# A fourth pair of split buffers for the feed-forward, embedding, gated and MLP stages of a two-model forward pass

## What is computed

```
h = h + concat(diff_attention, gated_conv) @ a_w_out          # first model, layer 0
h = h + swiglu(rms_norm(h), ffn_w1, ffn_w3, ffn_w2)           # D_FF = 2816
h = h + sigmoid(rms_norm(h) @ ple_gate[0]) * (p[0] @ ple_proj[0])
u, v = split(gelu(rms_norm(h) @ c_w_in))                      # first model, layer 1
h = h + (u * (w_s @ layer_norm(v) + b)) @ c_w_out
h = h + moe_swiglu(rms_norm(h))                               # top 2 of 8 experts
h = h + sigmoid(rms_norm(h) @ ple_gate[1]) * (p[1] @ ple_proj[1])
for l in range(2):                                            # second model
    h = h + g1 * (concat(swa, mla, nsa, moba)(norm(h) @ w_in[l]) @ w_out[l])
    h = h + g2 * (square(relu(norm(h) @ w_up[l])) @ w_down[l])
```

## Time and profile before

| | |
|---|---|
| median of 3 runs | 1989.69 us (1988.63 to 1994.04) |
| profiled execution, first to last instruction | 1988.3 us |
| PE busy | 1911.1 us (96%) |
| DVE busy | 1555.3 us (78%) |
| ACT busy | 1197.3 us (60%) |
| mean granted TensorE clock | 0.988 of full speed |
| HBM read | 510.14 MB, 257 GB/s over the span |

### The profile page before, as it was taken

One profiled execution on the slowest core, in us unless ns is written; L12 is line 12 of the kernel. 1 busy time (PEld: TensorE's weight loads), 2 busy tenths in 40 slices (PEclk: granted clock), 3 DMA queues, 4 the chain that ended last, 5 costly groups with the idle time before them and its releaser, 6 DMA issues.

```text
span 1988.3 us, 27637 instructions
## 1 busy us (share of the span) xinstructions
PE 1911.1 (96%) x10878; PEld 1646.7 (83%) x10878; DVE 1555.3 (78%) x2130; ACT 1197.3 (60%) x1649; POOL 28.8 (1%) x32
## 2 busy tenths in 40 slices
PE   7999999999999999999999999889899999989998
PEld 7989998777888888888888888679789988978997
DVE  5768887667898989898989899567678985856555
ACT  4544435545777777777777778457554445654443
POOL 0010000000000000000000000000000000000000
PEclk9999999999999999999999999999999999999999
DMA  7348886535999999999989899533258883324551
GB/s 306 128 160 327 327 329 249 197 138 229 341 355 343 355 344 354 344 350 348 356 342 356 341 357 347 220 129 124 88 198 339 346 331 131 125 85 159 191 191 43
DMA packets 71694, 513.08 MB, mean 258 GB/s; under 512 B 8194, under 2 KB 8578, under 8 KB 10114
## 3 DMA queue, kind: packets, MB, share of 16 engines
q1 hardware_dynamic: 69536, 504.40, 67.3%
q10 hardware_dynamic: 2020, 6.82, 1.0%
HBM read 510.14 MB, written 1.05 MB: 257 GB/s over the span
## 4 chain that ended last, share of the span: by engine, by line
PE 88%; DVE 6%; ACT 4%; issue 1%; POOL 1%; DMA 0%; POOLq 0%; SPq 0%; ACTq 0%; DVEq 0%
PE ps L536 27%; PE ps L538 26%; PE ps L537 26%; PE ps L757 2%; DVE w_lo L1375 2%; ACT w_hi L2263 2%; PE ps L945 1%; PE ps L709 1%; PE ps L722 1%; PE ps L963 1%; POOL stat L2768 1%; DMA ring<-in_stream 0%; ACT xT L2273 0%; DVE y_lo L1998 0%; PE ps L992 0%
## 5 line engine op out<-in xcount | busy, mean ns | idle before, releaser
L2263 ACT ACTIVATE w_hi<-ring 128x1024 fp32r<-128x1024 f32 x862 | 911.9, 1061 | 632.7 <-PE ps L538 625.0
L1375 DVE TENSOR_TENSOR w_lo<-ring,w_hi 128x1024 fp32r<-128x1024 f32 x862 | 1041.8, 1223 | 301.4 <-ACT w_hi L2263 278.1
L536 PE MATMUL ps<-w_hi,x_hi 128*128 128x512 f32 (+1 forms) x1056 | 409.4, 390 | 8.8 <-DVE w_lo L1375 3.6
L538 PE MATMUL ps<-w_hi,x_lo 128*128 128x512 f32 (+1 forms) x1056 | 400.1, 381 | 0.0
L537 PE MATMUL ps<-w_lo,x_hi 128*128 128x512 f32 (+1 forms) x1056 | 399.3, 380 | 0.0
L536 PE MATMUL ps<-x_hi,w_hi 128*128 128x256 f32 x1248 | 359.8, 288 | 5.5 <-DVE x_lo L1490 4.5
L537 PE MATMUL ps<-x_lo,w_hi 128*128 128x256 f32 x1248 | 355.3, 285 | 0.0
L538 PE MATMUL ps<-x_hi,w_lo 128*128 128x256 f32 x1248 | 355.0, 284 | 0.0
L536 PE MATMUL ps<-w_hi,h_hi 128*128 128x512 f32 x732 | 289.8, 396 | 2.4 <-DVE h_lo L1983 2.4
L537 PE MATMUL ps<-w_lo,h_hi 128*128 128x512 f32 x732 | 285.3, 390 | 0.0
L538 PE MATMUL ps<-w_hi,h_lo 128*128 128x512 f32 x732 | 284.7, 389 | 0.0
(11 more groups left out here) (280 smaller groups left out, 1401.4 us busy)
## 6 DMA issues: line engine op xcount, KB each, us to landing
ring<-in_stream SPq DMA_DIRECT2D x479, 1024.0 KB, 5.0
con<-in_consts ACTq DMA_DIRECT2D x1, 2048.0 KB, 23.3
arena<-in_ln_rows ACTq DMA_DIRECT2D x3, 512.0 KB, 4.3
resid<-in_x SPq DMA_DIRECT2D x1, 1024.0 KB, 6.2
arena<-in_c ACTq DMA_DIRECT2D x2, 512.0 KB, 3.6
arena<-in_fin_row ACTq DMA_DIRECT2D x2, 512.0 KB, 4.2
out<-rows SPq DMA_DIRECT2D x2, 512.0 KB, 2.6
arena<-in_w_s ACTq DMA_DIRECT2D x1, 512.0 KB, 8.3
```

Source lines behind the costliest of these rows:

```text
L536: pe.matmul(out_, lhs[0], rhs[0], start=start, stop=False)
L538: return pe.matmul(out_, lhs[1], rhs[0], start=False, stop=stop)
L1375: dve.tensor_tensor(lo, ring[:, q % RING, a:a + HALF], hi.bitcast(F32), ALU.subtract)\
L2263: act.activation(half_buffer(m)[0], ring[:, q % RING, a:a + HALF], ACT.Copy).then_inc(hi_ready, 1)
```

## The change

The table `BUFFER` gets four pairs in the ranges of halves `DEEP` instead of in the experts' alone: 32 to 675, 702 to 771 and 798 to 861. In each range pairs are counted from the range's own start. Where a limit of `split_to` was a sum with `PAIRS`, it is now `reach(...)`. DVE gets one wait ahead of the scores of each block, for the last half in the fourth pair.

```
-MOE_PAIRS = 4
+DEEP_PAIRS = 4
+DEEP = (range(2 * W_FFN0, 2 * (W_BLK + B_V)), range(2 * (W_BLK + B_MLP), 2 * (W_BLK + B_ALL + B_V)),
+        range(2 * (W_BLK + B_ALL + B_MLP), 2 * SLOTS))
 def buffers_of_halves():
-    moe = range(2 * W_MOE, 2 * W_PLE1)
-    buffer = [(m - moe.start) % MOE_PAIRS if m in moe else m % PAIRS for m in range(2 * SLOTS)]
+    buffer = [m % PAIRS for m in range(2 * SLOTS)]
+    for stages in DEEP:
+        for m in stages:
+            buffer[m] = (m - stages.start) % DEEP_PAIRS
     held, before = {}, []
...
-                split_to(2 * done + PAIRS)
+                split_to(reach(2 * done))
                 dve.wait_ge(act_ready, ready(j))
...
                 split_to(reach(h0 + 12))
+                dve.wait_ge(half_done, h0 + 2 * B_V)
                 soften(0)
...
             split_to(2 * (W_OUT0 + 4) + 1)
-            norm_hi(1, 2 * (W_OUT0 + 4) + PAIRS)
+            norm_hi(1, reach(2 * (W_OUT0 + 4)))
...
-            square_rows(4, 2 * (W_COUT + 4) + PAIRS)
+            square_rows(4, reach(2 * (W_COUT + 4)))
...
-                norm_hi(6 + 2 * l, 2 * (n0 + B_IN) + PAIRS)
+                norm_hi(6 + 2 * l, reach(2 * (n0 + B_IN)))
...
-                norm_hi(7 + 2 * l, 2 * (n0 + B_MLP) + PAIRS)
+                norm_hi(7 + 2 * l, reach(2 * (n0 + B_MLP)))
```

More of the change, by code:

```diff
@@ L2499, in _ @@
             split_to(2 * W_PLE0 + 1)
-            norm_hi(2, 2 * W_PLE0 + PAIRS, lambda: keep_gates(0, (0, 1, 2, 3)))
+            norm_hi(2, reach(2 * W_PLE0), lambda: keep_gates(0, (0, 1, 2, 3)))
             ple(0)
             split_to(2 * W_CIN + 1)
-            norm_hi(3, 2 * W_CIN + PAIRS)
+            norm_hi(3, reach(2 * W_CIN))
             act.dma_start(ln_g, ln_rows[0].partition_broadcast(P)).then_inc(ln_in, 16)
@@ L2638, in embedding @@
                 split_end[0] = 2 * SLOTS
-                split_to(2 * W_PLE1 + PAIRS)
+                split_to(reach(2 * W_PLE1))
                 act.dma_start(ln_g, fin_row[0].partition_broadcast(P)).then_inc(fin_in, 16)
```

## The result

The changed kernel takes 1995.57 us (median of 7 runs, 1994.22 to 2000.78) against 1989.69 (7 runs beside them, 1988.63 to 1994.04). The ratio is 1.0036, 95% interval 1.0026 to 1.0046: slower by 7.2 us, 5.2 to 9.2 (the two medians alone differ by 5.9). The forecast was 1996.3, 6.65 us above the profiled execution of before. The profiled execution of the changed kernel took 1995.57 us, its first to last instruction 1993.8 (before: 1988.3), so the profile has 5.5 us to explain.

What follows compares the result with a forecast made beforehand. PE, busy 96% of the span, bounds the kernel, so only seams could move. Waits of +3.75 us plus clock +2.9 gave +6.65 on 1988.3, 1994.9; with 1.4 for the median, 1996.3 us, range 1995.3 to 1997.5.

Steps and rivals of the forecast that it cites:

- Inside FFN, MLP and embedding: Inside these stages PE never waits for splits, so a fourth pair changes nothing: 0 us.
- Gated stage: PE's waits for w_lo at 397.31, 405.09 and 418.65 shrink: -3.1 us, bounds -1.2 to -3.5.
- Norm before the FFN: Half 32 waits for 30 (1.36 us), 35 is split ahead of the squares (0.95): +2.3 us, bounds 0.95 to 2.3.
- The other norms: Extra splits ahead of the squares: +0.5 us before each MLP, +0.95 before block 1.
- Norm before the experts: The added split is offset because 132 leaves the place ahead of the first squares: 0 us.
- Half 772: Block 1's values projection: 772 shares pair 1 with 771 and must wait for it: +2.6 us, bounds 2.3 to 2.9.
- DVE's new wait: Stands where the scores it guards have already been waited for: 0 us.
- The sum without the clock: All waits together: -3.1 + 2.3 + 1.0 + 0.95 + 2.6 = +3.75 us.
- The clock: Granted clock falls after the pauses before the FFN (1.3 us) and in block 1 (1.6): +2.9 us, bounds 0 to 4.8.
- its rule: Clock at 0.50 after a pause of 2.2 us and more, no fall after 1.70 us; 1.6 us lost at 1270.
- The rule of that section which the prediction weighed: Half rate is TensorE's resting state, so a pause costs more than its length: +6.65, against +3.75 by waits alone.
- The rival on the other side: Clock holds at both pauses, before the FFN and in block 1: +3.75 us, 1993.4 us; chance 0.08.

Runs made afterwards that it cites:

- e6: Changed kernel with the pairs of halves 32 to 131 taken in order 2, 0, 1, 3, so half 32 waits for 29 again; 1996.49 us, ratio 1.0033.
- e1: Changed kernel with the old split limits in the norms before the FFN, both MLPs and block 1; 1992.19 us, ratio 1.0008 against the kernel before.
- e7: Changed kernel with the old limits in four norms and new pair orders for halves 32 to 131 and from 702 and 798; 1988.97 us, ratio 0.9996.
- e8: Kernel before with only the gated stage four pairs deep, and one split less ahead of the squares in the FFN, MLP and block 1 norms; 1987.29 us.
- e9: Kernel before with only the gated stage deep, and DVE's split moved behind the scaling in FFN and MLP norms, ACT unchanged; 1989.78 us, ratio 0.9996.
- e2: Changed kernel with pairs in order 0, 3, 1, 2 in the ranges from 702 and 798, so 772 waits for 768; 1994.06 us, ratio 1.0015.
- e3: Changed kernel with 28 instead of 18 spare matmuls of PE in the norm before the FFN; 1999.61 us, ratio 1.0045 against the kernel before.
- e5: The changed kernel itself run and profiled again, nothing altered; 1998.24 us, ratio 1.0039 against the kernel before.
- e10: On e8, DVE's split of the first new half also moved behind the scaling in the norms before block 0 and block 1; 1987.71 us, ratio 0.9987.

## Why the prediction was right

**Inside FFN, MLP and embedding: 0.** Right. The windows are as full as before, and the starts of PE's instructions keep their distance from 150 to 355 us within 0.1 us.

**Gated stage: -3.1.** Measured -3.27 and -3.28, between the bounds. The parts differ a little: 1.6 us were gained up to 400 us, as forecast, of which 0.4 belong to an earlier small wait; 0.46 at 405 and 1.09 at 418.65 stood against 0.35 and 1.1.

**Norm before the FFN: +2.3, of 1.36 and 0.95.** Measured +2.30, and e6 and e1 measured the parts at 1.35 and 0.94. **The other norms: +0.5, +0.5, +0.95.** Measured 0.48, 0.47 and 0.94. e1 took all of them away. That the norms wait for ACT is thereby shown for these four. **Norm before the experts: 0.** No pause of PE shows there before or after; e6 and e7, in which 132 does not come earlier, show what the offset was worth, 0.92 us. Besides, e8 and e9 add that POOL's root stands on the same chain, and that 0.91 of its 1.47 us, which the prediction took as a fixed length, are owed to DVE's split.

**Half 772: +2.6.** Measured +2.78, and e2 took it away alone.

**DVE's new wait: 0.** Ahead of the first scores of each block DVE waits 1.28 us for PE's products, in before and in both profiles of the changed kernel.

The sum without the clock was forecast as +3.75 and measured as +3.70; that it is so near is owed in part to two errors of 0.2 us, in the gated stage and at 772, which offset each other.

**The clock: +2.9, of 1.3 and 1.6.** The size came out, the places did not, so this part of the number is in part luck. Behind the pause of 2.77 us the clock fell in all three profiles that have it (the two of the changed kernel and e2), but it cost 0.55 to 0.7 us, not 1.3: at half the clock the transposes took 1.29 us longer in the first, and much of that disappeared in the wait of 0.48 us for the norm's result that had stood behind them anyway, and in the first short products. Behind half 772 it fell in four of five profiles (not in the first of the changed kernel; in e1, e3, e5 and e6). Against the first it cost 1.4 us in e5, 1.7 in e1 and 2.9 in e6, for a forecast of 1.6. The two places together cost 0.7 us in the first profile of the changed kernel and 2.0 in the second. Other stretches at 0.50, at places where the change alters no wait, came and went by up to 4.5 us in one place.

Two rows from which the prediction took its rule do not repeat. The row at 361.30 shows the pause of 1.79 us ahead of the gated stage alone; the window behind it, in before, is at 1.00:

```profile
363.20:366.40 3.20, 3.20 (x15) 2.63 (x16) 3.10 (x13) 1.98 (x7) 0.15 (x1) 1.00 1.02 312
```

In the first profile of the changed kernel the clock fell at the end of that pause. Behind the wait of 2.4 us at the end of the experts, where it had fallen in before, it held; in e5 it fell there. The windows of the first profile, then of e5:

```profile
364.10:367.50 3.40, 2.92 (x7) 2.37 (x8) 3.36 (x10) 2.34 (x7) 0.00 (x0) 0.50 0.99 304
1273.80:1277.20 3.40, 3.40 (x15) 2.83 (x16) 3.20 (x3) 0.38 (x1) 0.20 (x1) 1.00 0.64 239
```

```profile
1268.00:1271.40 3.40, 3.40 (x9) 2.62 (x9) 2.55 (x3) 0.00 (x0) 0.00 (x0) 0.50 0.92 330
```

Of the twelve profiles the clock is at 0.50 at the first place in eight, and behind the second in eight. So the rows give no length of a pause from which on it costs the clock, which is what the prediction read out of them.

By the ratio the change costs 7.2 us, of which 3.70 are waits. At equal clock it costs 3.0 to 3.2, and its 18 runs have a mean clock of 0.983 to 0.988 where before has mostly 0.988 and 0.989: the other part, some 3.5 to 4 us, goes with the clock. The single places that make it up were seen only in profiles of two executions. The Trainium skill (TensorE: Matmul & The Clock Gate, Part 1: The HAM clock gate) says of a kernel's start that how much of it runs at half rate varies from run to run; in the middle of a kernel the traces show the same, with 1.00 and 0.50 behind one wait. The rule of that section which the prediction weighed, that a pause costs more than its length, fits the time on the whole (7.2 us lie nearer to +6.65 than to the +3.75 of the waits alone), but not at each pause, as half 772 in the first profile and the wait behind the experts show.

The rival on the other side, that the clock holds at both pauses, occurred in neither of the two profiles of the changed kernel; that it holds at one did, in the first.

## What to carry to other kernels

Here more buffers helped only at the places where a consumer waited for the producer, and how far the producer then runs ahead is work moved in front of something else: look at what stands behind it in its queue, above all a reduction on which a stage's end depends. Where two numberings of buffers meet, list for each index which one it waits for; a half that waits for its neighbour paid for the whole chain of copy and difference here, 2.78 us, and the mend of one such place (e6) made another. Take the gain at the one place that waits (here one number, 0.17%) and leave the rest alone. Where the granted clock differs from run to run, compare runs at the same clock before a difference of a few us is put down to the change.

## What the runs showed of the hardware

A wait of microseconds on TensorE has no fixed price: after the same 2.6 us the clock was at 0.50 in four profiles and at 1.00 in one, and the runs of that one program lie between 1991.61 and 2000.78 us, the longer ones at the lower mean clock (1993.1 us at 0.988, 2000.8 at 0.983). Savings of 2 to 3 us in waits, exact to 0.1 us in the trace, were partly lost in this.

Shorter pauses did not always keep the clock up. Where DVE's split was moved behind the scaling (e8 to e10), the clock fell behind five of the six norms of the MLPs, with a pause of 0.31 to 0.33 us ahead of the transposes; in the nine other profiles it did so behind three of eighteen, with pauses of 1.23 to 1.72. The pause of 1.45 us behind the transposes was the same in all. The reason was not found.

The root of the second token tile, a one-column instruction of GpSimd, took 1.46 to 1.48 us beside a split of VectorE, in the norms before the FFN and the two MLPs of nine profiles, and 0.55 to 0.56 us in the same norms of e8, e9 and e10, where no split ran beside it.
